# Attention scores from split queries and keys in three one-pass products, and a rotation made by VectorE alone

## What is computed

```python
def _rope(x, cos, sin):
    x1, x2 = jnp.split(x, 2, axis=-1)
    return jnp.concatenate([x1 * c - x2 * s, x1 * s + x2 * c], axis=-1)

q = _rms_norm(q.reshape(n_batch, n, SWA_HEADS, SWA_HEAD_DIM), q_gain)
k = _rms_norm(k.reshape(n_batch, n, SWA_KV_HEADS, SWA_HEAD_DIM), k_gain)
if rotate:
    q, k = _rope(q, cos, sin), _rope(k, cos, sin)
s_ctx = jnp.einsum('bqhgd,bkhd->bhgqk', qb, kc).astype(jnp.float32)
s_win = jnp.where(allowed, jnp.einsum('bqhgd,bkhd->bhgqk', qb, kb).astype(jnp.float32), -jnp.inf)
```

## Time and profile before

| what | value |
|---|---|
| median of 3 runs | 3080.75 us (3080.58 to 3081.11) |
| profiled execution | 3080.93 us |
| its span, first to last instruction | 3079.1 us |
| TensorE busy | 3039.5 us, 99% |
| VectorE busy | 1895.3 us, 62% |
| ScalarE busy | 1320.9 us, 43% |
| GpSimd busy | 100.1 us, 3% |

### The profile page before, as it was taken

How to read it: one execution, slowest core, us unless ns; L and a number is a source line. 1 busy time by engine, 2 the same in 40 slices (tenths; PEclk the granted TensorE clock), 3 DMA queues, 4 the chain that set the end, 5 groups by cost and what they waited for, 6 DMA issues and landing times.

```text
span 3079.1 us, 52667 instructions
## 1 busy us (share of the span) xinstructions
PE 3039.5 (99%) x21054; PEld 2611.0 (85%) x21054; DVE 1895.3 (62%) x2808; ACT 1320.9 (43%) x2247; POOL 100.1 (3%) x106
## 2 busy tenths in 40 slices
PE   9999999999999999999999999999999999999999
PEld 8897889889888988888788788788887888886999
DVE  6745575675447656776777477467735676367544
ACT  5544454554345453222464567432224222255533
POOL 0000000100000020000000000100000000000000
PEclk9999999999999999999999999999999999999999
DMA  7543554454345543554422000235522454221453
GB/s 267 189 151 137 188 184 175 171 186 176 143 159 181 186 166 134 194 193 164 151 80 96 2 4 3 97 148 194 194 106 82 166 213 180 89 89 42 140 188 123
DMA packets 62488, 441.24 MB, mean 143 GB/s; under 512 B 6768, under 2 KB 8944, under 8 KB 9328
## 3 DMA queue, kind: packets, MB, share of 16 engines
q1 hardware_dynamic: 60992, 437.39, 38.9%
q10 hardware_dynamic: 1328, 1.46, 0.1%
HBM read 437.77 MB, written 1.05 MB: 143 GB/s over the span
## 4 chain that ended last, share of the span: by engine, by line
PE 90%; DVE 5%; ACT 3%; issue 1%; POOL 0%; DMA 0%; DVEq 0%; ACTq 0%; SPq 0%; POOLq 0%
PE ps_high L544 46%; PE ps_low L544 42%; PE ps_low L553 1%; DVE sb_w_split L834 1%; ACT sb_w_split L797 1%; DVE sb_arena L2215 0%; ACT sb_xn L2900 0%; ACT sb_arena L2909 0%; PE ps_high L553 0%; DVE sb_x_split L3003 0%; DVE sb_silu L3023 0%; DVE sb_arena L5056 0%; DMA sb_ring<-weights 0%; DVE sb_rinv L4960 0%; DVE sb_xn L4381 0%
## 5 line engine op out<-in xcount | busy, mean ns | idle before, releaser
L797 ACT ACTIVATE sb_w_split<-sb_ring 128x2048 fp32r<-128x2048 f32 x260 | 498.5, 1917 | 891.1 <-PE ps_low L544 697.9
L834 DVE TENSOR_TENSOR sb_w_split<-sb_ring,sb_w_split 128x2048 fp32r<-128x2048 f32 x260 | 597.6, 2298 | 255.7 <-ACT sb_w_split L797 255.7
L544 PE MATMUL ps_low<-sb_x_split,sb_w_split 128*128 128x512 f32 (+1 forms) x3640 | 709.2, 352 | 8.9 <-DVE sb_w_split L834 4.0
L544 PE MATMUL ps_high<-sb_x_split,sb_w_split 128*128 128x512 f32 (+1 forms) x3544 | 690.9, 353 | 0.3 <-DVE sb_w_split L834 0.3
L544 PEld LDWEIGHTS ps_low<-sb_x_split,sb_w_split 128*128 128x128 f32 x3640 | 595.1, 189 | 110.8 <-DVE sb_x_split L3003 6.3
L544 PEld LDWEIGHTS ps_high<-sb_x_split,sb_w_split 128*128 128x128 f32 x3544 | 583.7, 189 | 94.7 <-DVE sb_w_split L834 0.6
L544 PE MATMUL ps_low<-sb_a_split,sb_w_split 128*128 128x256 f32 (+1 forms) x2112 | 370.2, 325 | 0.3 <-DVE sb_w_split L834 0.3
L544 PE MATMUL ps_high<-sb_a_split,sb_w_split 128*128 128x256 f32 (+1 forms) x2112 | 365.7, 323 | 0.0
L544 PEld LDWEIGHTS ps_low<-sb_a_split,sb_w_split 128*128 128x128 f32 x2112 | 314.2, 190 | 37.9 <-DVE sb_w_split L834 2.6
L544 PEld LDWEIGHTS ps_high<-sb_a_split,sb_w_split 128*128 128x128 f32 x2112 | 314.9, 190 | 30.9
L1047 DVE SCALAR_TENSOR_TENSOR sb_rest<-sb_ring,sb_consts 128x1024 f32<-128x1024 f32 x256 | 313.3, 1224 | 26.0 <-DVE sb_rest L1047 6.2
(11 more groups left out here) (443 smaller groups left out, 3137.2 us busy)
## 6 DMA issues: line engine op xcount, KB each, us to landing
sb_ring<-weights SPq DMA_DIRECT2D x412, 1024.0 KB, 4.8
sb_consts<-consts SPq DMA_DIRECT2D x1, 2148.0 KB, 18.4
sb_sq<-xT SPq DMA_DIRECT2D x1, 1024.0 KB, 5.6
sb_ring<-weights SPq DMA_DIRECT2D x2, 512.0 KB, 7.6
sb_h<-ctxT ACTq DMA_DIRECT2D x1, 1024.0 KB, 14.4
out<-sb_h SPq DMA_DIRECT2D x1, 512.0 KB, 3.0
sb_vectors<-vectors ACTq DMA_DIRECT2D x1, 269.0 KB, 5.8
out<-sb_h SPq DMA_DIRECT2D x1, 256.0 KB, 2.7
```

The source lines that it names most:

```text
L544: ins = self.g.nc.tensor.matmul(out, lhsT, rhs, start=start, stop=stop)
L797: g.nc.scalar.activation(g.w_split[:, 0, s % 2, :], g.ring[:, n % SLOTS, :], ACT.Copy).then_inc(g.sem["w_high"], 1)
L834: g.nc.vector.tensor_tensor(g.w_split[:, 1, s % 2, :], g.ring[:, n % SLOTS, :], g.w_split[:, 0, s % 2, :].bitcast(F32), ALU.subtract).then ...
```

## The change

The sine table gets a minus sign on the rows of `x2`. A rotation on VectorE is now: four multiplications, each of 32 rows by 512 columns, that read 32 rows of a head and of the table and write the product on the 32 rows of the other half; one multiplication of all 128 rows by the cosine, with the table read twice by a stride of zero; one sum. The five rotation products of TensorE, and its waits for evicted queries, are gone; VectorE waits itself for the evictions.

Rotated queries and keys are then split: ScalarE writes their high parts (`turned_queries`, and one copy of 1024 columns for the keys), VectorE the low parts (`turned_low`). The queries' parts lie in one of the two slots for split weights, the keys' in one half of `a_split`, and the weights of the output projection use the other slot instead of that half. The scores of a group are six one-pass products on 64 partitions, the two heads in turn, and the mask products as before. TensorE waits for `turned_low`.

The order changes with it: half 9 of the input weights is split before the keys; `value_tile(1)` comes before `scores(0)`, and its eviction before the first exponentials; the low parts of the first two pairs of queries and of the keys stand between the keys' rotation and the first maxima on VectorE; `low_queries(2)` stands ahead of the fourth rotation and `low_queries(3)` behind `peaks(1)`. ScalarE's high parts of the last two stand among the evictions of value tiles.

```diff
@@ -198,7 +198,7 @@
...
     put("swa_cos", np.tile(np.cos(ang).T, (4, 1)))
-    put("swa_sin", np.tile(np.sin(ang).T, (4, 1)))
+    put("swa_sin", np.tile(np.concatenate([np.sin(ang).T, -np.sin(ang).T]), (2, 1)))
     keep = np.zeros((P, 2, TOK))
@@ -4579,16 +4579,28 @@
...
-SECOND_FROM = 1
+SECOND_FROM, ROTATED = 1, SWA_DIM // 2
 OUT_AT, OUT_SPACES, OUT_EARLY = 6, 3, (2, 4, 6)
...
-def swa_out_split(g, n):
+def swa_out_split(g, splits, n):
...
         return [g.x_split[:, 0, :, TOK + part * P:TOK + (part + 1) * P] for part in range(2)]
-    return [g.a_split[:, 2 - space, part, :, :].rearrange("p a (b n) -> p (a b) n", n=P) for part in range(2)]
+    if space == 1:
+        return [g.w_split[:, part, 1 - splits % 2, 0:CHUNK // 2].rearrange("p (k n) -> p k n", k=KT) for part in range(2)]
+    return [g.a_split[:, 0, part, :, :].rearrange("p a (b n) -> p (a b) n", n=P) for part in range(2)]
+
+
+def split_queries(g, splits, part):
+
+    return g.w_split[:, part, splits % 2, :].rearrange("p (n t) -> p n t", n=PAIRS)
+
+
+def split_keys(g, part):
+
+    return g.a_split[:, 1, part, :, :]
@@ -4667,14 +4679,13 @@
...
-    def open_query(n, side):
+    def open_query(side):
         pe.wait_ge(g.sem[side + "_free"], pe.tiles[side] - 3)
-        evicted[n] = (side, pe.tiles[side] + 1)
         return pe.open(side)
...
         for half in range(2):
-            w, tile = in_ready(2 * n + 2 + half), open_query(2 * n + half, "low")
+            w, tile = in_ready(2 * n + 2 + half), open_query("low")
             for k in range(KT):
@@ -4704,21 +4715,11 @@
...
-    def rotation(source):
-        pe.mm(pe.open("high")[:, :], g.const("rotate"), source, full="high")
-
-    def rotated_queries(n):
-        pe.wait_ge(g.sem["high_free"], pe.tiles["high"] - 3)
-        for half in range(2):
-            side, count = evicted[2 * n + half]
-            pe.wait_ge(g.sem[side + "_free"], count)
-        rotation(b["q"][:, 2 * n:2 * n + 2, :])
-
...
     key_tiles = [pe.open("low"), pe.open("low")]
-    query_tiles = [open_query(0, "low"), open_query(1, "high")]
+    query_tiles = [open_query("low"), open_query("high")]
     stream_tensor(pe, key_tiles[0], 3)
@@ -4748,41 +4749,36 @@
...
     length_sum(1)
-    rotated_queries(0)
     queries(2)
     query_lengths(0)
-    rotated_queries(1)
     identity, mask = exact_mask(g)
...
             pe.wait_ge(g.sem["mask_ready"], 1)
-        pe.wait_ge(g.sem["rotated"], pe.due("rotated", {0: 3, 4: 1, 6: 1}.get(p, 0)))
+        pe.wait_ge(g.sem["turned_low"], pe.due("turned_low", {0: 3, 4: 1, 6: 1}.get(p, 0)))
         for q in range(2):
...
             tiles = []
-            for i, head in enumerate(swa_pairs()[p]):
-                base, kv = SWA_DIM * i, head // (SWA_HEADS // SWA_KV)
+            for i in range(2):
                 pe.wait_ge(g.sem[side + "_free"], pe.tiles[side] - 3)
                 tiles.append(pe.open(side))
-                pe.mm(tiles[i][:, :], b["q"][base:base + SWA_DIM, p, q * P:(q + 1) * P],
-                      b["k"][base:base + SWA_DIM, kv // 2, :], True, False)
+            for n, (q_part, k_part) in enumerate(((0, 0), (0, 1), (1, 0))):
+                for i, head in enumerate(swa_pairs()[p]):
+                    rows, kv = slice(SWA_DIM * i, SWA_DIM * (i + 1)), head // (SWA_HEADS // SWA_KV)
+                    pe.mm(tiles[i][:, :], split_queries(g, pe.splits, q_part)[rows, p, q * P:(q + 1) * P],
+                          split_keys(g, k_part)[rows, kv // 2, :], n == 0, False)
             for i in range(2):
...
     queries(3)
-    pe.wait_ge(g.sem["high_free"], pe.tiles["high"] - 3)
-    pe.wait_ge(g.sem["dn_normed"], pe.due("dn_normed", 2))
-    rotation(b["k"][:, :, 0:TOK])
     query_lengths(1)
     value_tile(0)
+    value_tile(1)
     scores(0)
-    value_tile(1)
-    rotated_queries(2)
     value_tile(2)
-    rotated_queries(3)
     value_tile(3)
@@ -4857,8 +4853,7 @@
...
-    def query_root(half, skipped):
-        act.skip("high", skipped)
+    def query_root(half):
         act.wait_ge(g.sem["high_full"], act.tiles["high"] + 1)
@@ -4883,11 +4878,21 @@
...
     A(mask, g.const("swa_mask"), ACT.Copy).then_inc(g.sem["mask_ready"], act.adds("mask_ready"))
-    query_root(0, 1)
+    def turned_queries(n):
+        act.wait_ge(g.sem["turned"], act.due("turned"))
+        pair = slice(2 * n, 2 * n + 2)
+        A(split_queries(g, act.splits, 0)[:, pair, :], b["q"][:, pair, :], ACT.Copy).then_inc(g.sem["turned_high"], 1)
+
+    query_root(0)
     query(6)
     query(7)
-    query_root(1, 2)
+    turned_queries(0)
+    turned_queries(1)
+    query_root(1)
+    act.wait_ge(g.sem["turned"], act.due("turned"))
+    A(split_keys(g, 0), b["k"], ACT.Copy).then_inc(g.sem["turned_high"], 1)
     evict(b["v"][:, 0, :], 256, "high")
+    evict(b["v"][:, 1, :], 256, "high")
@@ -4901,11 +4906,10 @@
...
     exponentials(0)
-    evict(b["v"][:, 1, :], 256, "high")
-    act.skip("high")
     evict(b["v"][:, 2, :], 256, "high")
-    act.skip("high")
+    turned_queries(2)
     evict(b["v"][:, 3, :], 256, "high")
+    turned_queries(3)
     for p in range(PAIRS):
@@ -4942,11 +4946,15 @@
...
                     between=lambda k: swa_in_low(dve, 3 + k // 4, dve.chunks, dve.splits) if k in (0, 4) else None)
-    for n in range(5, 9):
+    for n in range(5, 10):
         swa_in_low(dve, n, dve.chunks, dve.splits)
+    queries_low, queries_high = dve.freed["low"] + 2, dve.freed["high"]
     dve.skip("low", PAIRS + 1)
...
+
+    def both(table):
+        return table.rearrange("p (o t) -> p o t", o=1).to_broadcast([P, 2, TOK])
@@ -4966,25 +4974,26 @@
...
-    def rotate(parts):
-        dve.wait_ge(g.sem["high_full"], dve.tiles["high"] + 1)
-        tile = dve.tile("high")
-        for half, raw in enumerate(parts):
-            v.tensor_tensor(raw, raw, cos, ALU.mult).then_inc(g.sem["vec_step"], dve.adds("vec_step"))
-            ins = v.tensor_tensor(b["tmp"][:, half, :], tile[:, half * TOK:(half + 1) * TOK], sin, ALU.mult)
-            if half:
-                ins.then_inc(g.sem["high_free"], dve.frees("high"))
-            else:
-                ins.then_inc(g.sem["vec_step"], dve.adds("vec_step"))
-        dve.wait_ge(g.sem["vec_step"], dve.made["vec_step"])
-        dve.wait_ge(g.sem["high_free"], dve.freed["high"])
-        for half, raw in enumerate(parts):
-            ins = v.tensor_tensor(raw, raw, b["tmp"][:, half, :], ALU.add)
-            if half:
-                ins.then_inc(g.sem["rotated"], dve.adds("rotated"))
-            else:
-                ins.then_inc(g.sem["vec_step"], dve.adds("vec_step"))
+    def rotate(raw):
+        other = b["tmp"]
+        for at in range(0, P, ROTATED):
+            to, rows = slice(at, at + ROTATED), slice(at ^ ROTATED, (at ^ ROTATED) + ROTATED)
+            v.tensor_tensor(other[to, :, :], raw[rows, :, :], both(sin)[rows, :, :],
+                            ALU.mult).then_inc(g.sem["vec_step"], dve.adds("vec_step"))
         dve.wait_ge(dve.last_sem, dve.last_count)
+        v.tensor_tensor(raw, raw, both(cos), ALU.mult).then_inc(g.sem["vec_step"], dve.adds("vec_step"))
+        dve.wait_ge(dve.last_sem, dve.last_count)
+        v.tensor_tensor(raw, raw, other, ALU.add).then_inc(g.sem["turned"], dve.adds("turned"))
+        dve.wait_ge(dve.last_sem, dve.last_count)
+
+    def turned_low(n, high, low, raw):
+        dve.wait_ge(g.sem["turned_high"], n + 1)
+        v.tensor_tensor(low, raw, high.bitcast(F32), ALU.subtract).then_inc(g.sem["turned_low"], 1)
+
+    def low_queries(n):
+        pair = slice(2 * n, 2 * n + 2)
+        high, low = (split_queries(g, dve.splits, part)[:, pair, :] for part in range(2))
+        turned_low(n if n < 2 else n + 1, high, low, b["q"][:, pair, :])
@@ -4999,7 +5008,10 @@
...
     def rotate_queries(n):
-        rotate([b["q"][:, 2 * n + half, :] for half in range(2)])
+        if n == 0:
+            dve.wait_ge(g.sem["high_free"], queries_high + 1)
+        dve.wait_ge(g.sem["low_free"], queries_low + max(1, 2 * n + 1))
+        rotate(b["q"][:, 2 * n:2 * n + 2, :])
@@ -5008,12 +5020,14 @@
...
     query_scales(0)
-    swa_in_low(dve, 9, dve.chunks, dve.splits)
     rotate_queries(1)
...
         swa_in_low(dve, n, dve.chunks, dve.splits)
-    rotate([b["k"][:, m, 0:TOK] for m in range(2)])
+    rotate(b["k"][:, :, 0:TOK])
+    low_queries(0)
+    low_queries(1)
     query_scales(1)
+    turned_low(2, split_keys(g, 0), split_keys(g, 1), b["k"])
@@ -5059,13 +5073,13 @@
...
     negated(0, reduced[0])
-    dve.skip("high", 2)
     rotate_queries(2)
     inverse_totals(0, read[0])
-    dve.skip("high")
+    low_queries(2)
     rotate_queries(3)
-    dve.skip("high")
+    dve.skip("high", 4)
     read[1], reduced[1] = peaks(1)
+    low_queries(3)
     for p in range(PAIRS):
```

10 lines of the change are left out of this document (5 added, 5 removed).

## The result

The changed kernel takes 3088.51 us, the median of 13 runs (3087.76 to 3090.77); the kernel before took 3081.42 us in as many runs beside it (3080.49 to 3083.15). The ratio is 1.0023 with a 95% interval of 1.0016 to 1.0031: 7.1 us slower. That it is slower is clear of the noise; whether it passes 0.2%, which the prediction took as its bound for no change, the interval leaves open. The range held it; the forecast of 3083.5 us was 5 us too low, 0.5 of it because the kernel before came to 3081.4 in these runs and not 3080.9.

The account below looks back on a forecast made before the run. TensorE, the chain's end for 90% of the span, was taken to bound the kernel. Row products 5.2 us later, less 2.6 us back in the loop, gave +2.6 on 3080.9: 3083.5 us, range 3078.5 to 3092.0.

Parts of the forecast that it names:

- the steps of the forecast: VectorE's work ahead of the first copy of probabilities moves the first row products from 2800.30 to 2805.5: +5.2 us.
- cover: Before the first scores, 1.1 us of TensorE's wait for VectorE in which slower value tiles cost nothing.
- six pairs shorter: In the loop over pairs, 0.43 us less for each of the six scores left: 2.6 us back.
- the two waits: TensorE waits for VectorE 4.9 us before the value tiles and 5.1 us before the first row products.
- S: Start of the first scores, forecast for 2787.7, 5.5 us later than in the kernel before.
- (3): In VectorE's rotations, writing across groups of rows costs double: 12.5 us more, 3096 us; chance 0.06.
- (4): On VectorE, 32-row instructions are short or the work hides; TensorE keeps its 9.1 us: 3071.8 us; chance 0.12.
- The middle: A rotation on VectorE taken as 4.13 us, between 3.97 and 4.30: 1.8 us more than before, five times.
- rival (2): In the scores, the heads of one-pass products don't run side by side: +10.4 us, 3091.3 us; chance 0.08.
- pairs slower than 7.1: Sign against the forecast: pairs in the loop after the first row products running slower than 7.1 us.
- the clock: TensorE's clock falls after long waits: one +4.3 or +5.5 us, both +7.2; chance 0.18 (scores unchanged included), both 0.11.
- The price from the kernel's start: A clock fall costs 2.85 us, taken from TensorE's slower records after idling, until 7.08 us.

Follow-up runs that it names:

- e2_split_early: Kernel before with one edit, half 9 of the input weights split ahead of the keys: 3079.26 us, ratio 0.9994.
- e4_no_cross: Changed kernel with each of the four multiplications writing the 32 rows it reads, halves not exchanged: 3088.99 us, one execution.
- e5c_row_pairs: Changed kernel with each 32-row multiplication cut in two of 256 columns, one after another on the same rows: 3089.89 us, one execution.
- e7_old_scores: Changed kernel with scores back in plain float32 products, without high and low parts of queries and keys: 3088.59 us, ratio 1.0023.
- e6_tensor_rot: Changed kernel with the rotation left to TensorE and VectorE's old rotation, as in the kernel before: 3077.14 us, ratio 0.9986.
- e1_busy: Changed kernel with idle TensorE products, 11 ahead of the first value tile and 9 ahead of the first pair's transposes: 3086.65 us, ratio 1.0014.
- e3_one_mult: Changed kernel with one multiplication of 128 rows in place of the four of 32, halves not exchanged: 3079.32 us, ratio 0.9989.
- e9_late_rotation: Changed kernel with the fourth rotation and the low parts beside it moved later on VectorE, into the loop over pairs: 3082.57 us, ratio 1.0004.

## Why the prediction was right or wrong

The change is slower, as forecast, but by 7.1 us where the sum had 2.6. Up to 6.2 us counted as no change in the prediction, which gave that 0.66 and slower 0.26. The sum by its terms, in us, as forecast and as the profile of the changed kernel has it:

| term | forecast | measured |
|---|---|---|
| row products later, by the steps of the forecast | +5.2 | +5.2 |
| key rotation starts later (2769.77 for 2769.55) | 0 | +0.22 |
| five rotations of 4.32 instead of 4.13 | 0 | +0.95 |
| value tiles at the low clock, beyond their cover | 0 | +1.15 |
| rest | 0 | +0.15 |
| row and value products at the low clock | 0 | +1.33 |
| six pairs shorter | -2.6 | -2.0 |
| sum | +2.6 | +7.0 |

**Right: where TensorE ends late.** The prediction put the two waits at the splits of weights and at the first copy of probabilities, with 4.9 and 5.1 us; both are 5.33. The squares' wait was put at some 0.6 and is 0.56. First scores were given for 2787.7; VectorE was ready for them at 2788.52, and TensorE, held by its value tiles, began them at 2789.67. The step from S to the row products was 17.8 and is 18.3, two rotations of 0.19 and 0.12 more. So TensorE's savings before the row products are swallowed whole, as said. Half 9 costs nothing ahead of the keys to within 0.11 us (the first reciprocal at 2761.17 for 2761.06), and `e2_split_early` shows what it was worth alone: 1.2 us in the profile.

**Right: 32 rows take as long as 128, and writing on other rows is free.** Rivals (3) and (4) are out: `e4_no_cross` for the one, 4.32 us for the other. The Trainium skill (Vector Engine (DVE) Microarchitecture Reference, section 3.8) says so of moves across quadrants; `e4_no_cross` agrees, with 2.82 against 2.83 us.

**The middle was taken where the end was the answer.** The four multiplications went at the dependent pace and the rotation at the upper end of 3.97 to 4.30, and 0.02 us over. The Trainium skill (VectorE: DVE Perf Modes, "Two Vector instructions with no wait between them") had been quoted for this in the prediction, and the sum left it aside for want of a row; `e5c_row_pairs` agrees with it, with 0.44 us at a change of rows and 0.34 without. It cost 0.95 us of the 4.4 that the sum lacked.

**The scores: mechanism right, size a little high.** The heads run side by side in one-pass products: six records of a group within 0.96 us, so rival (2) is out. But a group takes 1.26 us (2789.67 to 2790.93) where 1.43 was and 1.22 was forecast: 0.17 saved, not 0.21, and 0.33 a pair, not 0.43. Six pairs give 2.0. `e7_old_scores` and `e6_tensor_rot` bear out the 0.33. A pair takes 7.21 us, and pairs slower than 7.1 were one of the prediction's own signs that it would be wrong: that sign came.

**Wrong: the clock.** It was a rival, with 0.29 for one fall or two (scores left unchanged among them), and held down by "nothing in this trace shows a fall at all". That was weak evidence: the longest wait in that trace was 1.5 us, and the one place where TensorE came out of a longer rest, the start, did show the low level in the spacing of its records (0.43 and then 0.22 us), though the granted clock of the profile reads 1.00 there. The clock was low behind both long waits in the profile of the changed kernel, and the mean clock was 0.998 there and 1.000 before. This is the largest missing term, 2.5 us by the profile; `e1_busy` got 1.9 of it back with a fall of its own left in.

The rival's number, 7.2 us for both falls, is the measured one, but partly by luck. It took 1.75 us for the first fall and 2.85 for the second, 4.6 in all; they cost 1.15 and 1.33. Of the 10.2 us of the first low stretch 4.8 lay in the wait itself. The tiles lost 2.41 us (8.31 for 5.90), and of these 1.26 fell into the cover (the tiles at full clock would have ended at 2787.26, VectorE at 2788.52). The second ended soon after the work began again. The price from the kernel's start was too high, and the terms above made up the difference.

## What to carry to other kernels

Moving work off the bounding engine gains only if the engine that takes it is not late at the next handover: five rotation products cost TensorE 4.3 us (0.86 each, by the prediction's estimate) and 11.4 us once they were VectorE's, since each of its rotations stood in front of something that TensorE waited for. Moving one of them back, with two low parts, gave 5.9 us. A wait of TensorE is to be priced with the slower work behind it, and a trace without long waits says nothing against that. Of a change in several parts, the parts are worth timing alone: scores, early split and value tile order made the kernel 4 us faster without the rotation, of which the early split alone is 1.2 us in the profile. The value tile order alone was not timed.

## What the runs showed of the hardware

- TensorE's clock fell to its lower level behind or in waits of 2.45 (`e3_one_mult`), 3.70 (`e7_old_scores`, 0.50 from 2807 to 2810) and 5.33 us. The fall came 0.6 and 4.7 us after TensorE had stopped in the changed kernel, and only 1.3 to 1.4 us after it had begun again in `e1_busy`, `e3_one_mult` and `e9_late_rotation`. The length of one wait doesn't decide it: it didn't fall behind the 1.5 us of the kernel before, and did behind 1.45 us in `e9_late_rotation`, and in `e1_busy` at 2791.0 after waits of 0.51 and 1.30 us with filler products ahead of them. What decides there, the runs don't show. The Trainium skill (TensorE: Matmul & The Clock Gate, "What's actually happening") says that throttled is the default and activity releases it; the low stretches behind long waits agree; that sentence alone doesn't foretell the fall in `e1_busy`. A fall cost 1.15 and 1.33 us in the changed kernel.
- On VectorE, an instruction that starts on other rows than the one before it starts 0.72 us after it at 512 columns, where 0.60 is the step of independent ones of 128 rows, and 0.44 instead of 0.34 at 256. 32 rows by 512 took 0.68 us, as long as 128 rows.
- Six 64-row one-pass products of 512 columns, for two heads in turn, take 0.17 us a group less than two plain float32 products (1.26 for 1.43), where three passes for four at 0.216 would give 0.21.
